# A pair of squares added on GpSimd ahead of the sums that TensorE makes for an RMS norm

## The chip, the core and the metric

The kernel runs on one core of a Trainium2 chip. The metric is the device time of one execution in microseconds. The core has five engines with instruction queues of their own, which meet only at semaphores: TensorE (PE in the profile; PEld is its weight load), VectorE (DVE), ScalarE (ACT), GpSimd (POOL) and SyncE (SP), which issues most of the DMAs.

## What is computed

Two small models in a row, for one sequence of 256 tokens of width 1024: two hybrid layers (latent attention, a gated delta rule and block attention side by side), a last norm, and then four layers, each with a feed-forward part, a mixer (HGRN2, mLSTM, sliding-window attention, HGRN2), a second feed-forward part and a gated projection. Ahead of each of these parts stands an RMS norm. What the change touches is the mean of squares in it:

```python
def rmsnorm_2(x, gain):
    xf = x.astype(jnp.float32)
    y = xf * lax.rsqrt(jnp.mean(xf * xf, axis=-1, keepdims=True) + EPS)
    return (y * gain.astype(jnp.float32)).astype(x.dtype)

def swiglu(x, w_gu, w_down):
    g, u = jnp.split(x @ w_gu, 2, axis=-1)
    return (jax.nn.silu(g) * u) @ w_down
```

Everything is in float32.

## The kernel before

The activations lie transposed: `x` is 128 partitions (of the width) by 8 tiles by 256 tokens. All products with weights are made in three matmuls of 128x128 by 256, from a high and a low part of either operand (`with_hi`, `with_lo`, L137 to L146). The weights come in 781 chunks of 512 KB through a ring; ACT makes the high part of a chunk (`hi`, L92), DVE the low part (`lo`, L100), five chunks ahead of TensorE.

A norm isn't waited for. TensorE multiplies the unscaled `x` times gain, and the root of the mean square scales the product afterwards. On the way from the residual `x` to that root (class `Norm` and the four functions behind it):

- ACT squares the tiles of `x` into `xn` (`square`, L219), right behind the high part of each tile (`split_hi`, L206).
- DVE adds the squares of tiles 0 to 5 down to one tile in three steps (`fold_six`, L246, L250, L253).
- TensorE sums over the partitions: `sum_squares` (L370) takes each 128x128 half of a tile of squares as weights, with a column of ones as the moving operand. It sums three tiles: 0, 6 and 7. A matmul of plain float32 stands in the trace as two records, so three tiles of two halves are 12 records.
- ACT takes the mean (`root_in`, L383), GpSimd the power -0.5 (`spread_root`, L397), TensorE spreads it over the partitions (`rstd_rows`, L410), and DVE copies it (`take_rstd`, L418). Then DVE scales the first product (L555), ACT makes the SiLU (L527), DVE the product (L559), ACT its high part (L531), DVE its low part (L564), for which the first down-projection `down` waits (L452).

Norms with the sum of three tiles follow a `finish` of `OutProjection` (six: one per hybrid layer and one per mixer) and a `ple` with a next layer (three). The one behind the second hybrid layer also serves the last norm of the first model: class `Inner` squares `x` a second time, folds it and sums another three tiles (L323). The other norms square in two big pieces and sum one tile; they aren't touched.

The order on each engine is the order in which the functions write their blocks. On GpSimd that is, behind a mixer's out-projection: `split_p` (L618, a cast, and L620, a subtraction, both 128x512, for the gated projection far behind), and then the power of `spread_root`. `split_p` is written after the out-projection, but waits only for things that are long done there.

## Time and profile before

| | us |
|---|---|
| median of 3 runs | 2420.28 |
| lowest, highest | 2419.44, 2424.91 |
| profiled execution, its own time | 2427.05 |
| span of the profiled execution | 2425.2 |

The engines' busy times are TensorE 2410.8 us, DVE 1725.1, ACT 1317.8 and GpSimd 91.4. In the rows, a number such as L370 is the line of the kernel; times count from the start of the span. The granted clock of TensorE is at its full level in all 40 slices of the span. TensorE's matmuls overlap: a record of a matmul of 256 columns is 0.28 us long, while the next starts 0.11 us after it, so distances between starts count there, not lengths.

### The profile page before, as it was taken

Reading aid. Unit: us, or ns where it says so; the run is one execution under the profiler, and the core shown is the slowest. Engines: PE = TensorE matmul, PEld = TensorE weight load, DVE = VectorE, ACT = ScalarE, POOL = GpSimd, SP = SyncE. Lnnn points to the kernel's source line nnn. Section 1 sums busy time; section 2 is a strip of 40 time slices with the busy share of each in tenths; the row PEclk is TensorE's granted clock in tenths of the full one; section 3 lists DMA queues with packets and bytes.
Section 4 is the critical chain, followed back from the end, with each engine's and each line's share of the span. In section 5 each row is a group of like instructions: output and inputs, shape, how many; then the busy total and the mean of one; then the engine's idle time right before and its main releaser. Section 6 shows DMA issues by size and latency. Waiting matters only on the chain.

```text
span 2425.2 us, 51808 instructions
## 1 busy us (share of the span) xinstructions
PE 2410.8 (99%) x20462; PEld 2381.4 (98%) x20462; DVE 1725.1 (71%) x2422; ACT 1317.8 (54%) x2019; POOL 91.4 (4%) x91
## 2 busy tenths in 40 slices
PE   9999999999999999999999999999999999999999
PEld 9999999999999999999999999998999999999999
DVE  8878867568776677667766676687667766877666
ACT  5756755446564465445544554466445544765444
POOL 1000000001200000000000000000000000220000
PEclk9999999999999999999999999999999999999999
DMA  7315326555456556655465566543655655535563
GB/s 267 114 62 174 122 67 221 183 185 170 131 174 194 190 180 201 195 185 182 136 203 188 170 210 196 191 140 124 203 194 178 197 197 191 166 123 190 191 194 127
DMA packets 115378, 418.86 MB, mean 173 GB/s; under 512 B 12832, under 2 KB 14112, under 8 KB 114976
## 3 DMA queue, kind: packets, MB, share of 16 engines
q1 hardware_dynamic: 114096, 412.40, 52.2%
q8 instruction: 109, 1.79, 0.3%
q0 software_dynamic: 560, 2.10, 0.3%
q10 hardware_dynamic: 576, 2.27, 0.2%
q14 instruction: 37, 0.30, 0.0%
HBM read 414.62 MB, written 2.10 MB: 172 GB/s over the span
## 4 chain that ended last, share of the span: by engine, by line
PE 94%; DVE 3%; ACT 1%; DMA 0%; issue 0%; ACTq 0%; SPq 0%; DVEq 0%
PE ps_gu L140 18%; PE ps_gu L146 17%; PE ps_gu L141 17%; PE ps_acc L140 9%; PE ps_acc L146 8%; PE ps_acc L141 8%; PE ps_acc L2709 1%; PE ps_acc L2270 1%; PE ps_misc L140 1%; DVE w_lo L100 1%; PE ps_gu L2306 1%; PE ps_misc L141 1%; PE ps_misc L146 1%; PE ps_sum L140 1%; PE ps_sum L146 1%; PE ps_sum L141 1%
## 5 line engine op out<-in xcount | busy, mean ns | idle before, releaser
L100 DVE TENSOR_TENSOR w_lo<-w_raw,w_hi 128x1024 fp32r<-128x1024 f32 x781 | 953.2, 1228 | 382.6 <-ACT w_hi L92 377.8
L140 PE MATMUL ps_gu<-xn_hi,w_hi 128*128 128x256 f32 x3832 | 1057.9, 280 | 2.2 <-DVE x_res L1342 0.8
L141 PE MATMUL ps_gu<-xn_hi,w_lo 128*128 128x256 f32 x3832 | 1047.0, 277 | 0.0
L92 ACT ACTIVATE w_hi<-w_raw 128x1024 fp32r<-128x1024 f32 x781 | 819.7, 1056 | 362.7 <-PE ps_gu L146 269.1
L146 PE MATMUL ps_gu<-xn_lo,w_hi 128*128 128x256 f32 x3832 | 1010.7, 277 | 0.0
L140 PEld LDWEIGHTS ps_gu<-xn_hi,w_hi 128*128 128x128 f32 x3832 | 719.9, 188 | 5.8 <-issue 2.5
L141 PEld LDWEIGHTS ps_gu<-xn_hi,w_lo 128*128 128x128 f32 x3832 | 720.2, 188 | 0.3
L146 PEld LDWEIGHTS ps_gu<-xn_lo,w_hi 128*128 128x128 f32 x3832 | 697.3, 188 | 0.0
L140 PE MATMUL ps_acc<-h_hi,w_hi 128*128 128x256 f32 x1496 | 415.1, 278 | 0.0
L146 PE MATMUL ps_acc<-h_lo,w_hi 128*128 128x256 f32 x1496 | 413.6, 276 | 0.0
L141 PE MATMUL ps_acc<-h_hi,w_lo 128*128 128x256 f32 x1496 | 413.5, 276 | 0.0
L527 ACT ACTIVATE silu<-ps_gu 128x256 f32<-128x256 f32 x176 | 67.7, 384 | 425.8 <-DVE ps_gu L555 425.8
L140 PEld LDWEIGHTS ps_acc<-h_hi,w_hi 128*128 128x128 f32 x1496 | 280.7, 188 | 0.3
L146 PEld LDWEIGHTS ps_acc<-h_lo,w_hi 128*128 128x128 f32 x1496 | 280.8, 188 | 0.0
L141 PEld LDWEIGHTS ps_acc<-h_hi,w_lo 128*128 128x128 f32 x1496 | 280.8, 188 | 0.0
L555 DVE TENSOR_TENSOR ps_gu<-ps_gu,rstd 128x512 f32<-128x512 f32 x176 | 123.0, 699 | 62.0 <-PE ps_gu L146 61.7
L559 DVE TENSOR_TENSOR h<-silu,ps_gu 128x256 f32<-128x256 f32 x176 | 74.1, 421 | 90.0 <-ACT silu L527 90.0
L140 PE MATMUL ps_acc<-xn_hi,w_hi 128*128 128x256 f32 x336 | 95.1, 287 | 0.5 <-DVE xn L3422 0.5
L141 PE MATMUL ps_acc<-xn_hi,w_lo 128*128 128x256 f32 x336 | 92.1, 278 | 0.0
L397 POOL TENSOR_TENSOR rstd_columns<-mean_square_columns,powers 128x2 f32<-128x2 f32 x17 | 18.9, 1112 | 1891.6 <-ACT mean_square_columns L383 1891.6
L146 PE MATMUL ps_acc<-xn_lo,w_hi 128*128 128x256 f32 x336 | 87.0, 278 | 0.0
L564 DVE TENSOR_TENSOR h_lo<-h,h_hi 128x256 fp32r<-128x256 f32 x176 | 74.0, 420 | 7.7 <-ACT h_hi L531 7.7
(462 smaller groups left out, 2637.6 us busy)
## 6 DMA issues: line engine op xcount, KB each, us to landing
w_raw<-in_w_dram SPq DMA_DIRECT2D x781, 512.0 KB, 4.1
const<-in_const_dram SPq DMA_DIRECT2D x1, 1216.0 KB, 8.6
distance_rows<-arena POOLq DMA_DIRECT2D x1, 1024.0 KB, 6.5
p_all<-distance_rows POOLq DMA_DIRECT2D x2, 512.0 KB, 5.3
p_all<-in_p_dram ACTq DMA_DIRECT2D x1, 1024.0 KB, 6.4
out_dram<-x_res SPq DMA_DIRECT2D x8, 128.0 KB, 1.9
x_res<-in_x_dram ACTq DMA_DIRECT2D x1, 512.0 KB, 6.7
x_res<-in_x_dram SPq DMA_DIRECT2D x1, 512.0 KB, 6.1
```

Source lines behind the costliest of these rows:

```text
L92: act.activation(self.w_hi[:, s, :], self.w_raw[:, r, :], ACT.Copy).then_inc(self.w_hi_ready.sem, 1)
L100: dve.tensor_tensor(self.w_lo[:, s, :], self.w_raw[:, c % NR, :], self.w_hi[:, s, :], ALU.subtract)\
L140: pe.matmul(out, self.w_hi[:, s, j0:j0 + width], rhs_hi, start=start, stop=False, skip_group_check=True)
L141: pe.matmul(out, self.w_lo[:, s, j0:j0 + width], rhs_hi, start=False, stop=False, skip_group_check=True)
L146: return pe.matmul(out, self.w_hi[:, s, j0:j0 + width], rhs_lo, start=False, stop=last, skip_group_check=True)
L527: act.activation(k.s[:, t % 2, :], k.ps_gu[t % 2][:, 0:S], ACT.Silu).then_inc(silu.sem, 1)
L555: dve.tensor_tensor(gu, gu, k.rstd[:, :].unsqueeze(1).to_broadcast([P, 2, S]), ALU.mult).then_inc(sc.sem, 1)
L559: dve.tensor_tensor(k.h[:, t % 2, :], k.s[:, t % 2, :], k.ps_gu[t % 2][:, S:2 * S], ALU.mult)\
L564: dve.tensor_tensor(k.h_lo[:, t % 2, :], k.h[:, t % 2, :], k.h_hi[:, t % 2, :], ALU.subtract)\
L2270: mm = pe.matmul(at_bank(acc01, n), four(Lm[lv % 2])[:, n, :], four(T)[:, n, :], start=(n % 4 == 0), stop=True, skip_group_check=True)
L2306: mm = pe.matmul(gub(n), four(U)[:, n, :], four(Y)[:, n, :], start=(n % 4 == 0), stop=True, skip_group_check=True)
L2709: mm = pe.matmul(ps[:, h * P:(h + 1) * P], lhs(h), rhs(h), start=(h == 0), stop=True, skip_group_check=True)
```

## The change

The diff below is shortened. The squares of tiles 6 and 7 are added on GpSimd into tile 6 (`fold_pair`), as soon as the last square is made, and `sum_squares` sums tiles 0 and 6. It waits for that addition (`pair_folded`) in place of the squares. `Inner` gets the same. The new blocks are written behind the out-projection or the gated projection, and so ahead of `split_p`.

```diff
-        self.tiles = (0,) if squares < KD else (0, 6, 7)
+        self.tiles = (0,) if squares < KD else (0, 6)
...
+    def fold_pair(self):
+        k, xn = self.k, self.k.xn
+        @k.block.gpsimd
+        def _(pool):
+            pool.wait_ge(*k("square_made").at(self.squares))
+            pool.tensor_tensor(xn[:, 6, :], xn[:, 6, :], xn[:, 7, :], ALU.add).then_inc(*k("pair_folded").up())
+
     def made(self):
-        self.k.take(self.b, self.h0, self.l0, 1)
-        self.k.summed = self.tiles, self.k("square_made").at(self.squares)
+        k = self.k
+        k.take(self.b, self.h0, self.l0, 1)
+        if len(self.tiles) == 1:
+            k.summed = self.tiles, k("square_made").at(self.squares)
+        else:
+            self.fold_pair()
+            k.summed = self.tiles, k("pair_folded").made()
...
+    def fold_pair(self):
+        k, squares = self.k, self.squares
+        @k.block.gpsimd
+        def _(pool):
+            pool.wait_ge(*k("inner_square_made").at(KD))
+            pool.tensor_tensor(squares[:, 6, :], squares[:, 6, :], squares[:, 7, :], ALU.add)\
+                .then_inc(*k("inner_pair_folded").up())
     def sum(self, pe):
...
-        pe.wait_ge(*k("inner_square_made").at(KD))
-        for m in (0, 6, 7):
+        pe.wait_ge(*k("inner_pair_folded").at(1))
+        for m in (0, 6):
...
         nxt.made()
+        if inner:
+            inner.fold_pair()
```

TensorE, at the sum behind a gated projection (`ps_gu0` and `ps_gu1` are the banks of the first two feed-forward tiles), before:

```order
L146 MATMUL ps_gu0<-xn_lo1,w_hi 128x256 [waits xn_lo_ready]
L146 MATMUL ps_gu0<-xn_lo1,w_hi 128x256
L370 MATMUL ps_sum<-ones,xn 128x1 [waits square_made,squares_folded,misc_free]
L370 MATMUL ps_sum<-ones,xn 128x1 x5
L140 MATMUL ps_gu1<-xn_hi1,w_hi 128x256 [waits w_lo_ready,ple_gate_ready]
```

and after the change:

```order
L146 MATMUL ps_gu0<-xn_lo1,w_hi 128x256 [waits xn_lo_ready]
L146 MATMUL ps_gu0<-xn_lo1,w_hi 128x256
L394 MATMUL ps_sum<-ones,xn 128x1 [waits pair_folded,squares_folded,misc_free]
L394 MATMUL ps_sum<-ones,xn 128x1 x3
L140 MATMUL ps_gu1<-xn_hi1,w_hi 128x256 [waits w_lo_ready,ple_gate_ready]
```

Two of six matmuls (four of twelve records) are gone, and the wait is for the addition in place of the squares.

GpSimd, behind the second mixer (mLSTM), before; `rstd_columns` is the power of `spread_root`, once for the norm ahead of the mixer and then for the one behind it:

```order
L397 TENSOR_TENSOR rstd_columns<-mean_square_columns,powers 128x2 [waits mean_sq_col]
L613 UNCONDITIONAL_BRANCH
L618 CAST h_hi<-p_all 128x512 [waits chunk_done,p_loaded]
L620 TENSOR_TENSOR h_lo<-p_all,h_hi 128x512 [waits p_hi_ready]
L391 UNCONDITIONAL_BRANCH
```

and after the change:

```order
L421 TENSOR_TENSOR rstd_columns<-mean_square_columns,powers 128x2 [waits mean_sq_col]
L242 UNCONDITIONAL_BRANCH
L245 TENSOR_TENSOR xn<-xn 128x256 [waits square_made]
L637 UNCONDITIONAL_BRANCH
L642 CAST h_hi<-p_all 128x512 [waits chunk_done,p_loaded]
L644 TENSOR_TENSOR h_lo<-p_all,h_hi 128x512 [waits p_hi_ready]
L415 UNCONDITIONAL_BRANCH
```

The addition stands ahead of the cast and the subtraction of `split_p`, with a wait for the last square. These two follow it from now on, at all four mixers.

## Rows read from the trace of the kernel before

**Rows 1.** The page: busy times, and the chain that ended last by engine

```profile
PE 2410.8 (99%) x20462; PEld 2381.4 (98%) x20462; DVE 1725.1 (71%) x2422; ACT 1317.8 (54%) x2019; POOL 91.4 (4%) x91
PE 94%; DVE 3%; ACT 1%; DMA 0%; issue 0%; ACTq 0%; SPq 0%; DVEq 0%
```

**Rows 2.** Waits of TensorE, first of twelve: us in total, times, longest

```profile
PE ps_sum L140 <- ACT xn_hi L1235: 2.1, 2, 1.0
```

**Rows 3.** Instructions of L370: ns min/median/max, first and last start, form

```profile
L370 PE MATMUL ps_sum<-ones,xn x144: 164/250/250, 17.8 to 2402.0; 128*128 128x1 f32 x144
```

**Rows 4.** Timeline of TensorE, inner sum: start us, us, line, operation, out<-in, count

```profile
376.24 1.48 PE L323 MATMUL ps_sum<-ones,arena 128*128 128x1 f32 x12
377.58 0.36 PE L140 MATMUL ps_gu<-xn_hi,w_hi 128*128 128x256 f32 x1
```

**Rows 5.** Groups by form, POOL and DVE: busy us, mean ns, idle before

```profile
L2256 POOL TENSOR_TENSOR arena<-arena,const 128x1024 f32<-128x1024 f32 x4 | 9.5, 2372 | 177.5 <-PE ps_acc L2270 177.5
L100 DVE TENSOR_TENSOR w_lo<-w_raw,w_hi 128x1024 fp32r<-128x1024 f32 x781 | 953.2, 1228 | 382.6 <-ACT w_hi L92 377.8
```

**Rows 6.** Timelines of POOL and DVE, at the first and second split_p

```profile
642.45 0.61 POOL L618 CAST h_hi<-p_all 128x512 fp32r<-128x512 f32 x1
643.14 1.69 POOL L620 TENSOR_TENSOR h_lo<-p_all,h_hi 128x512 fp32r<-128x512 f32 x1
643.00 0.68 DVE L2692 TENSOR_TENSOR arena<-arena 128x512 f32<-128x512 f32 x1
643.59 2.32 DVE L100 TENSOR_TENSOR w_lo<-w_raw,w_hi 128x1024 fp32r<-128x1024 f32 x1
1101.85 1.30 POOL L620 TENSOR_TENSOR h_lo<-p_all,h_hi 128x512 fp32r<-128x512 f32 x1
```

**Rows 7.** Timelines behind the first gated projection: ACT, DVE, PE, PEld

```profile
912.32 0.40 ACT L219 ACTIVATE xn<-x_res 128x256 f32<-128x256 f32 x1
913.90 0.43 DVE L253 TENSOR_TENSOR xn<-xn 128x256 f32<-128x256 f32 x1
914.25 4.62 DVE L100 TENSOR_TENSOR w_lo<-w_raw,w_hi 128x1024 fp32r<-128x1024 f32 x4
918.88 0.42 DVE L418 COPY rstd<-ps_sum 128x256 f32<-128x256 f32 x1
921.39 0.42 DVE L564 TENSOR_TENSOR h_lo<-h,h_hi 128x256 fp32r<-128x256 f32 x1 [0.48 <-ACT h_hi L531]
915.35 1.39 PE L370 MATMUL ps_sum<-ones,xn 128*128 128x1 f32 x12
922.33 0.19 PEld L140 LDWEIGHTS ps_acc<-h_hi,w_hi 128*128 128x128 f32 x1
```

**Rows 8.** Timelines behind the first mixer's out-projection: ACT, DVE, PEld

```profile
701.35 0.40 ACT L219 ACTIVATE xn<-x_res 128x256 f32<-128x256 f32 x1
701.22 1.22 DVE L100 TENSOR_TENSOR w_lo<-w_raw,w_hi 128x1024 fp32r<-128x1024 f32 x1
702.35 0.69 DVE L250 TENSOR_TENSOR xn<-xn 128x512 f32<-128x512 f32 x1
702.96 0.48 DVE L211 SCALAR_TENSOR_TENSOR xn_lo<-x_res,vec,xn_hi 128x256 fp32r<-128x256 f32 x1
703.35 0.42 DVE L253 TENSOR_TENSOR xn<-xn 128x256 f32<-128x256 f32 x1
705.66 1.42 PEld L370 LDWEIGHTS ps_sum<-ones,xn 128*128 128x128 f32 x12
707.20 0.26 ACT L383 ACTIVATE mean_square_columns<-ps_sum,eps 128x2 f32<-128x2 f32 x1 [2.25 <-PE ps_sum L370]
708.45 1.23 DVE L100 TENSOR_TENSOR w_lo<-w_raw,w_hi 128x1024 fp32r<-128x1024 f32 x1 [2.41 <-ACT w_hi L92]
```

**Rows 9.** Timeline of DVE behind the two hybrid layers' sums

```profile
201.73 0.42 DVE L418 COPY rstd<-ps_sum 128x256 f32<-128x256 f32 x1 [5.26 <-PE ps_sum L410]
379.06 1.23 DVE L100 TENSOR_TENSOR w_lo<-w_raw,w_hi 128x1024 fp32r<-128x1024 f32 x1 [2.95 <-ACT w_hi L92]
```

## What the change should do to the time

> **What bounds the kernel now.** I read the page first: TensorE is busy for 2410.8 of 2425.2 us and holds 94% of the chain that ended last, while GpSimd works for 91.4 us [rows 1]. Then TensorE's own waits: twelve rows, the longest in total 2.1 us, about 10 us in all [rows 2]. So time that goes out of TensorE's queue is time of the kernel, unless TensorE then comes too early to something that another engine makes. That is read at each place of the change from timelines: when the last square ends, what DVE does until the root is there, and when the first down-projection wants its operand.
>
> **What is removed.** L370 has 144 records in 18 norms [rows 3]. Nine of these norms sum three tiles, 12 records each, and nine sum one, 4 records each: 108 and 36, which is 144. The inner norm has another 12 [rows 4]. The change takes 4 records out of each of ten sums, 40 in all. A record costs what it holds the next one back: 12 of them run from 376.24 to the 377.58 of the next L140, 1.34 us or 0.112 each [rows 4]. Four are 0.45 us, and 40 are **4.47 us**, if nothing gives any of it back. This is the bound above of the saving.
>
> **What is added.** Ten additions of 128x256 on GpSimd. No such row is in the trace. The nearest are the same operation with 1024 columns, 2.37 us [rows 5], and L620 with 512, 1.30 us where DVE leaves it alone [rows 6]. A straight line through the two gives 0.23 us and 1.07 per 512 columns, so 0.77 us for 256. GpSimd has nothing else to do there, and the sum comes 2.6 to 4 us behind the last square: 912.72 to 915.35 behind a gated projection [rows 7], 701.75 to 705.66 behind a mixer [rows 8]. By itself the addition is hidden everywhere.
>
> It isn't by itself, since DVE is at work in that stretch, and the two get in each other's way. Rows 6 show it. L620 of GpSimd wants to start at 643.14, when DVE's L2692 runs (until 643.68). It takes 1.69 us in place of 1.30, so it waits for L2692. DVE's next instruction, an L100 that begins at 643.59, takes 2.32 us in place of 1.228 [rows 5]: it is held for 1.09 us. All three read two operands from SBUF. So GpSimd gets its turn when DVE's running instruction ends, even with another of DVE's right behind, and holds that next one for its record less 0.21 us (1.30 - 1.09). For the new addition that is 0.77 - 0.21 = 0.56 us, about half of 1.09. For the cast (0.61 us) I estimate 0.40. A hold can't be below zero; its bound above is the whole record.
>
> **The three sums behind gated projections.** The last square ends at 912.72. DVE is busy without a gap from there to the copy of the root at 918.88 (the fold, then four L100 from 914.25 to 918.87), and from there the chain of the first feed-forward tile runs to the h_lo of L564, which ends at 921.81 [rows 7]. TensorE loads the first weights of that down-projection at 922.33. The slack is 0.52 us. Now TensorE comes 0.45 us earlier, at 921.88, and DVE 0.47 to 0.56 us later (the copy waited some hundredths for TensorE before), so h_lo is ready at 922.28 to 922.37. TensorE waits until then and starts where it started before. **0 us** each (between -0.1 and +0.02 with this hold), out of 0.45. What hid the addition was slack that the saving itself uses up. The fold ends at 914.33, and 914.9 is still ahead of the sum.
>
> **The four sums behind mixers.** Here DVE idles for 2.41 us ahead of the L100 at 708.45, because that waits for an ACT instruction which stands behind L383, and L383 waits for the sum [rows 8]. So the chain to the root starts from the sum and moves with it, and the down-projection sees no new slack or want. What can be late is the sum itself. The addition brings `split_p` behind it: three instructions on GpSimd in a row. They start at 701.8 and take turns with DVE. The addition gets in behind the L100 that ends at 702.44 and holds L250 by 0.56. The cast gets in behind L250 and holds L211 by 0.40. L620 gets in behind L211 and holds L253 by 1.09. L253, the last step of the fold, ended at 703.77 and now ends at 703.77 + 2.05 = 705.82. The sum loads its first weights at 705.66. It waits 0.16 us, so that 0.29 of 0.45 are left: **1.2 us** for four. DVE's two L100 behind the fold then end at about 708.2, just where the next one may start (708.45 less 0.29), so nothing more is lost. If one of the three falls into a gap of DVE, the loss is 0; hence 0 to 0.16.
>
> **The two sums of the hybrid layers.** DVE idles 5.26 us ahead of the root's copy in the first, and 2.95 us ahead of the next L100 in the second [rows 9]; both wait for things behind the sum. Nothing of `split_p` follows. The inner norm has two additions, 1.1 us of DVE, inside these 2.95. The saving stays: 0.45 for one sum and 0.89 for two. The fill of the arena with zeros (L1697, L1698) moves behind the first addition; it reads nothing, and is wanted only behind the root.
>
> **The sum**: 0.45 + 0.89 + 4 x 0.29 + 3 x 0 = 2.5 us. The profiled execution would have a span of 2422.7 in place of 2425.2, and an own time of 2424.5 in place of 2427.05. That execution lies 6.8 us above the median of the runs, 2420.28; I carry the difference over to the median: **2417.7 us**.
>
> **The rivals.**
>
> *All of it stays* (GpSimd's turns fall into DVE's gaps, or the copy at 918.88 has more room than it seems): 4.47 us, 2415.8. For it: DVE's instructions have gaps of some hundredths where a step of the fold waits for the last one. Against it: the row with 2.32 us. 20%.
>
> *The hold is dearer than the row.* If DVE is held for the whole GpSimd instruction, it is 0.77, 0.61 and 1.30 us. Behind gated projections the down-projection then starts 0.2 us later than before, 3 x -0.2. Behind mixers the fold ends at 703.77 + 2.68 = 706.45, 0.79 behind 705.66, so each loses 0.34. With 1.34 from the hybrid layers the sum is -0.7 us: 2421.0. Against it: 1.09 is less than 1.30 in the rows. 13%. The Trainium skill has this rule (SBUF — State Buffer, "Who interferes with whom"): a DVE instruction with two SBUF inputs and a GpSimd instruction that reads SBUF exclude each other, and the one that comes second is blocked until the other is through. By that page the change would gain nothing. The trace agrees with the exclusion, and its 1.09 us beside 1.30 says that the block is shorter than the instruction.
>
> *The saving comes back at every feed-forward part*, as a wait ahead of the first down-projection, and only the first sum, which no feed-forward part follows, keeps it: 0.45 us, 2419.8. Against it: the 2.41 us of idle DVE that end with the sum. 6%.
>
> *GpSimd finds no turn* (slower). If DVE keeps its operand path as long as it has the next instruction in its queue, the addition runs only when DVE's row of instructions ends. Behind a gated projection that is 918.87, and the sum is made at 919.4 in place of 915.24: 4.2 us, three times. Behind a mixer two L100 end at about 706.2, and the sum starts 1.1 us late, four times; the inner norm loses about 2. Together 12.6 + 4.4 + 2 - 4.5 = 14.5 us: 2434.8. It decides from where an addition waits for its turn for over 1.86 us behind a gated projection (2.63 us of room less its own 0.77). Against it: GpSimd did get in ahead of the L100 at 643.59. 5%.
>
> **How the numbers follow.** Forecast 56%, the rivals 20, 13, 6 and 5. A measurement of this kernel can tell about 0.2% from no change, 4.8 us, so faster begins at 2415.4. Faster: two in five of the first rival, whose 4.47 us lie just inside, and a little of the forecast by scatter, 12%. Slower: the last rival and a bit of the second, 6%. Within: 82%. The three runs before lie 5.5 us apart, so scatter counts beside the cases. The range takes in the first rival (2415.8) and the second (2421.0), 2415.0 to 2421.2, and leaves out the last and some scatter.
>
> **What would show it.** In the trace of the changed kernel: 8 records per touched sum, 16 for the two of the inner norm; the new addition at 0.77 us, or more where it waits; one DVE instruction behind it longer by 0.56; behind gated projections an h_lo that ends about 0.5 us later against the sum's start than before, and a short wait of TensorE ahead of `ps_acc`; behind mixers cast and subtraction ahead of the sum, L253 stretched by a microsecond, and the sum's first load waiting for it by 0.1 to 0.2 us; behind hybrid layers no wait. The prediction is wrong if DVE isn't stretched at all, if the additions end behind the sum's place, or if TensorE's rows outside these places change.

## The result and the profile after

The changed kernel takes **2448.95 us** (median of 15 runs, 2424.97 to 2458.14); the kernel before took 2424.16 us beside it (15 runs, 2416.88 to 2435.05). The ratio is 1.0087, with a 95% interval of 1.007 to 1.0104: slower by nearly 1%. The prediction, 2417.7 us (2415.0 to 2421.2), is wrong in sign, and the time lies far outside the range. The profiled execution took 2451.54 us with a span of 2449.7 us; it answers to the 2427.05 and 2425.2 of before.

The page of the changed kernel: busy times, the chain by engine, and TensorE's three groups of gate and up matmuls (the columns are those of [rows 1] and [rows 5]).

```profile
PE 2434.8 (99%) x20422; PEld 2403.9 (98%) x20422; DVE 1732.9 (71%) x2422; ACT 1318.3 (54%) x2019; POOL 105.8 (4%) x101
PE 92%; DVE 4%; ACT 2%; DMA 1%; issue 1%; POOL 0%; ACTq 0%; SPq 0%; DVEq 0%
L140 PE MATMUL ps_gu<-xn_hi,w_hi 128*128 128x256 f32 x3832 | 1065.3, 282 | 2.3 <-DVE x_res L1366 0.8
L141 PE MATMUL ps_gu<-xn_hi,w_lo 128*128 128x256 f32 x3832 | 1049.7, 278 | 0.0
L146 PE MATMUL ps_gu<-xn_lo,w_hi 128*128 128x256 f32 x3832 | 1013.8, 278 | 0.0
```

TensorE has the 40 records less that the change takes out (20462 in [rows 1]), and yet it is busy for 24.0 us more. No group of the page stands out: the three groups of 3832 have the same counts as before and means of 278 to 282 ns, and the idle column is as good as empty. The waits of TensorE hardly differ either. These are the first row, which is that of [rows 2], and the two rows that are new (us in total, times, longest):

```profile
PE ps_sum L140 <- ACT xn_hi L1259: 2.1, 2, 1.0
...
PE ps_sum L434 <- POOL rstd_columns L421: 0.6, 2, 0.3
...
PE ps_acc L140 <- DVE h_lo L588: 0.2, 1, 0.2
```

So 0.8 us of new waits stand beside 24.5 us of longer span. Where the time is can be seen if one counts TensorE's instructions in stretches of equal length, each in the middle of one of the eight feed-forward parts. The columns: the stretch, its us, then for PE, PEld, DVE, ACT and POOL the busy us with the number of instructions, then the granted clock, the DMA share and GB/s. First the kernel before (parts 1 to 4):

```profile
410.00:550.00 140.00, 140.00 (x1180) 140.00 (x1179) 84.11 (x100) 62.37 (x84) 0.00 (x0) 1.00 0.56 185
720.00:860.00 140.00, 140.00 (x1238) 140.00 (x1237) 88.57 (x105) 63.99 (x85) 0.00 (x0) 1.00 0.62 198
940.00:1080.00 140.00, 140.00 (x1238) 140.00 (x1237) 87.94 (x104) 65.35 (x88) 0.00 (x0) 1.00 0.62 195
1230.00:1370.00 140.00, 140.00 (x1238) 140.00 (x1237) 88.02 (x104) 64.43 (x87) 0.00 (x0) 1.00 0.61 193
```

and the changed kernel (all eight parts in their order):

```profile
400.00:540.00 140.00, 140.00 (x1237) 140.00 (x1237) 88.73 (x105) 65.59 (x88) 0.00 (x0) 1.00 0.61 199
720.00:860.00 140.00, 140.00 (x1179) 140.00 (x1179) 83.65 (x100) 61.69 (x83) 0.00 (x0) 1.00 0.56 185
940.00:1080.00 140.00, 140.00 (x1238) 140.00 (x1237) 88.18 (x104) 65.22 (x87) 0.00 (x0) 1.00 0.60 196
1230.00:1370.00 140.00, 140.00 (x1180) 140.00 (x1179) 83.66 (x100) 61.80 (x83) 0.00 (x0) 1.00 0.57 185
1440.00:1580.00 140.00, 140.00 (x1238) 140.00 (x1237) 89.26 (x105) 64.81 (x87) 0.00 (x0) 1.00 0.62 200
1720.00:1860.00 140.00, 140.00 (x1180) 140.00 (x1179) 84.73 (x99) 61.72 (x83) 0.00 (x0) 1.00 0.56 182
1930.00:2070.00 140.00, 140.00 (x1180) 140.00 (x1179) 84.82 (x99) 61.75 (x83) 0.00 (x0) 1.00 0.58 189
2260.00:2400.00 140.00, 140.00 (x1238) 140.00 (x1237) 88.36 (x105) 64.55 (x86) 0.00 (x0) 1.00 0.61 193
```

A part has one of two rates, and nothing between them: 1238 matmuls in 140 us, which is one in 113 ns, or 1180, one in 119. The granted clock is 1.00 in all of them, TensorE never idles, GpSimd does nothing there, and DVE, ACT and the DMA have slightly less to do in the slower ones, because TensorE asks for less. Before, one part of eight had the wide spacing (the first); after, four have it (parts 2, 4, 6 and 7). From the first SiLU of a part to its last, the 21 steps take 166.1 to 166.8 us at the narrow spacing and 174.0 to 174.7 at the wide one. Three more wide parts at 8.2 us are 24.6 us, and the span grew by 24.5. **The loss lies in the spacing of whole parts, not at the ten sums.** That the two numbers agree to a tenth is in part chance. Counted from the start of one norm's sum to the start of the next, a wide part is 8 to 9 us longer than a narrow one in the same place, and part 3 of the changed kernel, wide only at its beginning, is 0.9 us longer; against that stand some 1.6 us that the change does save, as the runs at the end show. The single times of the changed kernel show the groups too: they cluster at 2425, 2432, 2441, 2450 and 2458 us, in steps of about eight.

### The profile page after: what moved, and what is told of

Read it like the earlier page. It is cut to its first block, busy times and chain, and to the rows that moved or that the text cites. A ratio compares the mean times of both kernels' runs of the same rounds, so it can differ in the third digit from the quotient of the medians.

```text
span 2449.7 us, 51738 instructions
## 1 busy us (share of the span) xinstructions
PE 2434.8 (99%) x20422; PEld 2403.9 (98%) x20422; DVE 1732.9 (71%) x2422; ACT 1318.3 (54%) x2019; POOL 105.8 (4%) x101
## 4 chain that ended last, share of the span: by engine, by line
PE 92%; DVE 4%; ACT 2%; DMA 1%; issue 1%; POOL 0%; ACTq 0%; SPq 0%; DVEq 0%
PE ps_gu L140 17%; PE ps_gu L146 17%; PE ps_gu L141 17%; PE ps_acc L140 8%; PE ps_acc L146 8%; PE ps_acc L141 8%; PE ps_acc L2735 1%; DVE w_lo L100 1%; PE ps_acc L2296 1%; DMA w_raw<-in_w_dram 1%; PE ps_misc L140 1%; PE ps_gu L2332 1%; PE ps_misc L141 1%; PE ps_misc L146 1%; PE ps_sum L140 1%
## 5 line engine op out<-in xcount | busy, mean ns | idle before, releaser
L100 DVE TENSOR_TENSOR w_lo<-w_raw,w_hi 128x1024 fp32r<-128x1024 f32 x781 | 952.3, 1226 | 387.8 <-ACT w_hi L92 382.5
L140 PE MATMUL ps_gu<-xn_hi,w_hi 128*128 128x256 f32 x3832 | 1065.3, 282 | 2.3 <-DVE x_res L1366 0.8
L141 PE MATMUL ps_gu<-xn_hi,w_lo 128*128 128x256 f32 x3832 | 1049.7, 278 | 0.0
L140 PEld LDWEIGHTS ps_gu<-xn_hi,w_hi 128*128 128x128 f32 x3832 | 719.1, 188 | 6.1 <-issue 2.7
L141 PEld LDWEIGHTS ps_gu<-xn_hi,w_lo 128*128 128x128 f32 x3832 | 720.0, 188 | 0.3
L140 PE MATMUL ps_acc<-h_hi,w_hi 128*128 128x256 f32 x1496 | 419.3, 280 | 0.2 <-DVE h_lo L588 0.2
L141 PE MATMUL ps_acc<-h_hi,w_lo 128*128 128x256 f32 x1496 | 414.9, 277 | 0.0
L140 PEld LDWEIGHTS ps_acc<-h_hi,w_hi 128*128 128x128 f32 x1496 | 280.3, 187 | 1.2 <-DVE h_lo L588 1.0
L141 PEld LDWEIGHTS ps_acc<-h_hi,w_lo 128*128 128x128 f32 x1496 | 280.7, 188 | 0.0
L140 PE MATMUL ps_acc<-xn_hi,w_hi 128*128 128x256 f32 x336 | 94.8, 286 | 0.5 <-DVE xn L3448 0.5
L141 PE MATMUL ps_acc<-xn_hi,w_lo 128*128 128x256 f32 x336 | 92.0, 278 | 0.0
L588 DVE TENSOR_TENSOR h_lo<-h,h_hi 128x256 fp32r<-128x256 f32 x176 | 74.0, 420 | 7.7 <-ACT h_hi L555 7.7
```

The source lines that it names most:

```text
L100: dve.tensor_tensor(self.w_lo[:, s, :], self.w_raw[:, c % NR, :], self.w_hi[:, s, :], ALU.subtract)\
L140: pe.matmul(out, self.w_hi[:, s, j0:j0 + width], rhs_hi, start=start, stop=False, skip_group_check=True)
L141: pe.matmul(out, self.w_lo[:, s, j0:j0 + width], rhs_hi, start=False, stop=False, skip_group_check=True)
L588: dve.tensor_tensor(k.h_lo[:, t % 2, :], k.h[:, t % 2, :], k.h_hi[:, t % 2, :], ALU.subtract)\
```

## What the two spacings are

These are records of TensorE as read from the trace: start, line, distance to the record before it in ns, and by how much its weight load leads it. They follow the spreading of the root over the partitions (L410 before, L434 after), which comes some 3 us behind the sum: two matmuls of 128 columns that need the power of GpSimd. Behind the first mixer, before:

```
708.774 L146 d119 lead 116
708.889 L410 d115 lead  99    spreading, not waited for
708.997 L410 d108 lead 107
709.024 L140 d27  lead  25
709.227 L141 d203 lead 120
709.345 L146 d118 lead 115
709.462 L140 d117 lead 115
709.578 L141 d116 lead 113
709.692 L146 d114 lead 110
709.805 L140 d113 lead 110    from here 113, 114, 113 for 169 us
```

and after:

```
699.080 L146 d119 lead 116
699.234 L434 d154 lead   3    spreading, waited for
699.393 L434 d159 lead 107
699.421 L140 d28  lead  26
699.625 L141 d204 lead 120
699.751 L146 d126 lead 123
699.866 L140 d115 lead 112
699.984 L141 d118 lead 114
700.104 L146 d120 lead 118
700.222 L140 d118 lead 116    from here 117 to 120, now and then 124, for 187 us
```

In both kernels TensorE comes out of the sum at the wide spacing (the 119 in the first lines). The spreading ends that in the kernel before. Where TensorE has to wait for the spreading's operand, the wide spacing often stays, and then it stays to the end of the part. The wait itself is some hundredths of a microsecond here: the load starts 3 ns ahead of its matmul in place of 99, and the matmul comes 154 ns behind the record before it in place of 115. At parts 4, 6 and 8 this distance is 613, 505 and 176 ns. So parts 2, 4 and 6, which are wide, were waited for, and so was part 8, which is narrow. Part 7 is wide without a wait at its spreading (117 ns, load 98 ns ahead), and part 3 begins wide in the same way.

What made it wait is in the timelines of GpSimd and DVE behind the first mixer, after. Their counterparts before are [rows 8], and for the power the row that stands last here (from the kernel before):

```profile
692.40 1.20 POOL L245 TENSOR_TENSOR xn<-xn 128x256 f32<-128x256 f32 x1 [59.33 <-ACT xn L219]
693.56 1.07 POOL L642 CAST h_hi<-p_all 128x512 fp32r<-128x512 f32 x1
694.71 1.36 POOL L644 TENSOR_TENSOR h_lo<-p_all,h_hi 128x512 fp32r<-128x512 f32 x1
697.85 1.33 POOL L421 TENSOR_TENSOR rstd_columns<-mean_square_columns,powers 128x2 f32<-128x2 f32 x1 [1.78 <-ACT mean_square_columns L407]
...
691.79 1.22 DVE L100 TENSOR_TENSOR w_lo<-w_raw,w_hi 128x1024 fp32r<-128x1024 f32 x1
692.93 1.23 DVE L265 TENSOR_TENSOR xn<-xn 128x512 f32<-128x512 f32 x1
694.08 0.83 DVE L211 SCALAR_TENSOR_TENSOR xn_lo<-x_res,vec,xn_hi 128x256 fp32r<-128x256 f32 x1
694.83 1.52 DVE L268 TENSOR_TENSOR xn<-xn 128x256 f32<-128x256 f32 x1
696.27 3.71 DVE L100 TENSOR_TENSOR w_lo<-w_raw,w_hi 128x1024 fp32r<-128x1024 f32 x3
```

```profile
707.54 0.69 POOL L397 TENSOR_TENSOR rstd_columns<-mean_square_columns,powers 128x2 f32<-128x2 f32 x1 [62.71 <-ACT mean_square_columns L383]
```

The two engines take turns just as the prediction has it. The addition waits for the L100 that ends at 693.01. The fold's first step (L265, L250 before) takes 1.23 us in place of 0.69, so it is held for 0.54 (forecast 0.56); L211 0.83 in place of 0.48, 0.35 (0.40); the last step L268 1.52 in place of 0.42, 1.10 (1.09). The fold ends at 696.35 and the sum starts at 696.45, 212 ns behind the record before it where it was 116: a wait of 0.10 us (forecast 0.16). Then comes what the prediction left out: three L100 run without a gap from 696.27, and the **power** on GpSimd, two columns of numbers, is itself a reader of SBUF. It is free to go at 697.85, when the second L100 runs, and ends at 699.18, 1.33 us later in place of 0.69. At the second and third mixer it takes 1.79 and 1.68 us: it comes within 0.1 us of the start of an L100 and waits for all of it. TensorE, which comes 0.45 us sooner for its shorter sum, wants it at about 699.1.

## The experiments

Three theories. **W**: a wait of TensorE within a feed-forward part's first microseconds, however short, can leave it at the wide spacing for the whole part. **F**: the shorter sum does it, by its number of small matmuls. **G**: GpSimd's additions do it, by their use of SBUF. The first four kernels take the change apart and make W's wait with nothing of the change in it.

**Two tiles summed and no addition** (kernel before; the squares of tile 7 are left out of the mean):

```diff
-        self.tiles = (0,) if squares < KD else (0, 6, 7)
+        self.tiles = (0,) if squares < KD else (0, 6)
...
-        for m in (0, 6, 7):
+        for m in (0, 6):
```

> The kernel before, with the squares of tile 7 left out of the sums that take three tiles (the mean of squares is that of seven tiles): 8 records of small matmuls in place of 12 at ten places, no addition on GpSimd. In the trace of the changed kernel four of eight feed-forward parts run at 118.9 ns per matmul in place of 113.3 and are 8.2 us longer each; in that of before it is one. Theory W (a short wait of TensorE ahead of or behind the spreading of the root throws the part into the slow spacing): no wait arises here, so at most one or two parts are slow and the time is 3 to 5 us below before, ratio 0.998 to 0.9985. Rival F (it is the smaller number of small matmuls that leaves TensorE in the slow spacing): four parts slow, ratio about 1.01. Rival G (GpSimd's additions disturb): as W here.

Measured: 2425.5 us (12 runs, 2415.9 to 2441.99) beside 2419.8; ratio 1.0036 (1.001 to 1.0063). So all three theories missed: W and G forecast less time than before, and F four wide parts. The profiled execution (2424.9 us, span 2422.8) has one wide part, the third. A wait that I had not expected, and that the kernel before doesn't have, stands among TensorE's:

```profile
PE ps_sum L410 <- POOL rstd_columns L397: 0.5, 3, 0.2
```

It comes at the three sums behind gated projections. There the power is held by an L100 before as well. The power behind the first gated projection, before and with two tiles summed:

```profile
917.12 1.17 POOL L397 TENSOR_TENSOR rstd_columns<-mean_square_columns,powers 128x2 f32<-128x2 f32 x1 [24.31 <-ACT mean_square_columns L383]
```

```profile
906.49 1.62 POOL L397 TENSOR_TENSOR rstd_columns<-mean_square_columns,powers 128x2 f32<-128x2 f32 x1 [24.28 <-ACT mean_square_columns L383]
904.07 4.62 DVE L100 TENSOR_TENSOR w_lo<-w_raw,w_hi 128x1024 fp32r<-128x1024 f32 x4
```

It starts 0.45 us sooner against the four L100 and takes 0.45 us longer: the power ends when that L100 lets it, and TensorE, which arrives 0.45 us sooner than before, waits for it: its record comes 444 ns behind the last one. Three waits (parts 3, 5 and 7), one wide part: less than W in its strict form wants. But no part without a wait is wide, and five of the 12 runs lie at 2440.7 to 2442.0 us, some 26 above the 2415.43 that this kernel takes below with every profiled part narrow: by their time, all three parts were wide there. A shorter sum alone makes the kernel no faster, though it loses 40 records.

**Additions only**, three tiles still summed (changed kernel otherwise; the additions write a spare tile, and the sums wait for them as in the changed kernel):

```diff
-        self.tiles = (0,) if squares < KD else (0, 6)
+        self.tiles = (0,) if squares < KD else (0, 6, 7)
...
-            pool.tensor_tensor(xn[:, 6, :], xn[:, 6, :], xn[:, 7, :], ALU.add)
+            pool.tensor_tensor(k.spare[:, :], xn[:, 6, :], xn[:, 7, :], ALU.add)
```

> The kernel before with the ten additions on GpSimd, written into a spare tile, and TensorE waiting for them; the sums still take three tiles, 12 records. GpSimd's order is that of the changed kernel, cast and subtraction included. Theory W: the root behind the mixers is late by as much as in the changed kernel, less the 0.45 us by which TensorE comes later; the power there ends at 2.7 us behind the start of the sum, and TensorE wants it at 3.1, so it just isn't waited for, and the sums of the gated projections have their slack back: one to three slow parts, ratio 1.000 to 1.005. Rival G (the additions themselves slow the part): four slow parts, 1.01 to 1.015. Rival F: no more than before, 1.000.

Measured: 2450.66 us (6 runs, 2445.55 to 2464.36), ratio 1.0138 (1.0115 to 1.0161). Its page lists `PE ps_sum L439 <- POOL rstd_columns L426: 0.8, 3, 0.3` among TensorE's waits, again behind the gated projections, and the parts behind those three (3, 5, 7) are wide, all others narrow. The three waits are W's, but the time is what G had forecast (1.01 to 1.015) and W had not (up to 1.005): I had expected the gated projections' slack to cover the addition. F falls here: the number of small matmuls is that of before. G is left beside W, since the additions are in both.

**`split_p` written ahead of the mixer**, so that its cast and subtraction no longer stand behind the addition (changed kernel otherwise):

```diff
+            split_p(k, layer)
...
-            split_p(k, layer)
```

> The changed kernel, with split_p written ahead of the mixer in place of behind it, so that GpSimd has its cast and subtraction behind it when the addition comes. Theory W: behind the four mixers DVE is held by 0.56 us only, the power isn't late, TensorE doesn't wait at the spreading, and those four parts are fast; the three behind gated projections stay as in the changed kernel (one or two slow). Time 15 to 20 us below the changed kernel, ratio to before 1.000 to 1.004. Rivals F and G: as the changed kernel, 1.0087.

Measured: 2425.5 us (12 runs, 2416.66 to 2433.86), ratio 1.0025 (1.001 to 1.004), 23 us less than the changed kernel for the place of two instructions on GpSimd. All four parts behind mixers are narrow. In the profiled execution (span 2429.8) parts 1 and 5 are wide. TensorE waits for `h_lo` behind gated projections instead, `PE ps_acc L140 <- DVE h_lo L588: 1.6, 3, 0.6`. The two instructions haven't gone away: ahead of the mixer they stand right behind the power of the norm behind a gated projection, and there they hold DVE (these are the rows of part 3; in the changed kernel the four L100 take 4.62 us):

```profile
914.94 1.08 POOL L642 CAST h_hi<-p_all 128x512 fp32r<-128x512 f32 x1
916.10 2.16 POOL L644 TENSOR_TENSOR h_lo<-p_all,h_hi 128x512 fp32r<-128x512 f32 x1
912.06 5.04 DVE L100 TENSOR_TENSOR w_lo<-w_raw,w_hi 128x1024 fp32r<-128x1024 f32 x4
```

The wait for `h_lo` is about the same at the three places (the matmul behind it comes 858, 855 and 754 ns behind the last), and what it does is not: part 3 is narrow ahead of it and behind it, part 5 is narrow ahead and wide behind, part 7 wide ahead and narrow behind. The additions are all still there, so G can't be the whole of it.

**A late root and nothing else** (kernel before, with two fills of a spare tile on GpSimd between the mean and the power, at the eight feed-forward parts):

```diff
 def spread_root(k, n=None, late=False):
...
+        if late:
+            for _ in range(2):
...
+                pool.memset(k.spare[:, :], 0.0).then_inc(*k("spare_written").up())
...
-    spread_root(k)
+    spread_root(k, late=True)
```

> The kernel before, untouched but for two fills of a spare 128x256 tile on GpSimd between the wait for the mean and the power, at the eight feed-forward parts. Fills read nothing, so DVE isn't held; the root comes 0.6 to 0.8 us later. TensorE had 0.55 us of room behind mixers and some tenths behind gated projections, so it waits 0.1 to 0.8 us per part, 3 us in all. Theory W: four or more of eight parts fall into the slow spacing: 2450 us, ratio 1.008 to 1.02. Rivals F and G: only the waits themselves, ratio 1.001 to 1.002.

Measured: 2457.26 us (4 runs, 2456.38 to 2459.52), ratio 1.0151 (1.0134 to 1.0168). TensorE's wait and the stretches inside parts 3, 4 and 5:

```profile
PE ps_sum L415 <- POOL rstd_columns L402: 3.2, 4, 0.9
```

```profile
940.00:1080.00 140.00, 140.00 (x1180) 140.00 (x1180) 83.50 (x98) 61.20 (x81) 0.00 (x0) 1.00 0.57 185
1230.00:1370.00 140.00, 140.00 (x1238) 140.00 (x1237) 88.37 (x104) 64.30 (x86) 0.00 (x0) 1.00 0.59 193
1440.00:1580.00 140.00, 140.00 (x1180) 140.00 (x1179) 84.71 (x100) 62.22 (x83) 0.00 (x0) 1.00 0.58 187
```

Parts 3, 5, 7 and 8 are wide. No sum is shortened and nothing is added to anything, yet with 3.2 us of waits the kernel takes 37 us more. (A little of the profiled execution is another matter: from 370 to 390 us the granted clock is 0.80 and 0.86, with records 213 ns apart, the 1.2 GHz level, after 10 us in which TensorE was busy for 8.70. It costs about 3 us in part 1.) **That is W**: a late root is enough, without the shorter sum and without the additions. The kernel has two fills on GpSimd besides, ahead of every part. They aren't what decides: parts 2, 4 and 6 have them and are narrow, and the two tiles above have no fill and a wide part behind a wait. And a short wait alone isn't a sentence: at parts 2, 4 and 6 the matmul comes 143 or 144 ns behind the last in place of 115, and they stay narrow; part 8 (167 ns) and parts 3, 5 and 7 (1133 ns) turn wide.

**How often.** From the traces of seven kernels (before, after, the four above and the one with additions at mixers only, below), I took parts 2 to 8 and sorted them by whether the load of the spreading came 2 or 3 ns ahead of its matmul (it waited) or 60 to 99 ns (it didn't), and by the spacing of the records right behind:

```
                       narrow   wide
not waited for            29      3
waited for                 6     11
```

So a wait isn't a verdict but a draw, and it went the wrong way in about two of three, against one in eleven without it. The later wait for `h_lo` is a draw too, as the three parts with `split_p` first show. In the changed kernel it leaves part 5 narrow and part 7 wide. Part 3 comes out of the sum wide, stays so over a first wait for `h_lo`, and turns narrow within eight records behind a second one of 0.2 us at 930.2: a wait can also free it. The first part has two spreadings, its own and the inner norm's; among the seven kernels it ends wide in three (before, `split_p` first, additions at mixers only), with no wait at all. In these three the stream was narrow (113 ns) ahead of the first spreading and wide behind it, and one of the 3 in the table above, part 7 with `split_p` first, is the same case: the spreading that mostly ends a wide stretch begins one there.

**A way out of it.** This is an order of matmuls in which the wide spacing might not last. In tiles 1 and 2 of each part (the second and third), for the up-projection, the eight pairs with `xn_hi` are issued first and then the eight with `xn_lo` (the same matmuls in another order):

```diff
+                pairs = t in (1, 2) and n == 1
+                if pairs:
+                    for j in range(KD):
+                        k.with_hi(...)
                 for j in range(KD):
...
+                    if pairs:
+                        mm = k.with_lo(...)
+                        continue
```

I applied it to the kernel before, and to the kernel with the late root:

> The kernel before, with the matmuls of the up-projection in the second and third feed-forward tile in another order: first all sixteen with the high part of x, then the eight with its low part, as the first tile has them. The same matmuls, none more or less. In the traces so far the first tile nearly always runs at 113.3 ns, also where 118.9 came in. If this order is what brings the fast spacing back, no feed-forward part is slow (also the first, which is slow in the profile of before): 2415 to 2418 us, less scatter, ratio 0.997 to 0.999. If it doesn't matter: ratio 0.999 to 1.001 and the scatter of before.

> The same order of matmuls in the kernel with the late root (two fills ahead of the power), which ran at 2457 us. If the 37 us there are the slow spacing of whole feed-forward parts, this one falls to before plus the waits themselves: 2418 to 2425 us. If they come from the wait or from GpSimd in another way, it stays at 2450 or more. If the order of the matmuls doesn't bring the fast spacing back, it also stays.

Measured: before with this order, 2418.64 us (12 runs, 2416.43 to 2420.22) beside 2420.45, ratio 0.9987 (0.9976 to 0.9997), and its runs lie within 3.8 us where those of the kernel before beside it (33 runs) lie within 11.8. The median is 0.6 us over the range that I had given, the ratio is in it. The late root goes from 2457.26 to 2424.16 us (2421.32 to 2425.25), ratio 1.0004 (0.9992 to 1.0015). The same stretches of the late root with this order:

```profile
940.00:1080.00 140.00, 140.00 (x1237) 140.00 (x1237) 87.99 (x103) 64.27 (x86) 0.00 (x0) 1.00 0.59 193
1230.00:1370.00 140.00, 140.00 (x1237) 140.00 (x1237) 88.17 (x104) 63.98 (x85) 0.00 (x0) 1.00 0.59 193
1440.00:1580.00 140.00, 140.00 (x1238) 140.00 (x1237) 88.37 (x103) 63.98 (x85) 0.00 (x0) 1.00 0.60 194
```

TensorE still waits for the root there (2.6 us in three waits and 1.2 us in one). Beside the kernel before in the same order that is 5.5 us by the medians and 3.5 by the profiled spans (2419.2 and 2415.7). The 33 us between the two kernels with the late root are the spacing's: the fills and the waits are in both. How it turns is to be seen in the records of the changed kernel with this order, at the first part (start, line, distance, lead):

```
386.825 L141 d114 lead 112
386.944 L140 d119 lead 116
387.062 L141 d118 lead 115
387.180 L140 d118 lead 116
387.297 L141 d117 lead 114
387.417 L140 d120 lead 116
387.536 L141 d119 lead 115
387.649 L140 d113 lead 110    from here on 113, 113, 114
```

Six pairs of L140 and L141 pass at the wide spacing, then it falls to 113 inside the row of pairs.

**The change and its halves, with the draw taken out.** The same order on the changed kernel, on the sum without additions, on the additions without the sum, and on the changed kernel with `split_p` first:

> The changed kernel itself, with the order of matmuls that keeps every feed-forward part in the fast spacing; to be held against the kernel before with that order (2418.6 us). What is left is the change without its lottery: this is where the prediction's own sum, 2.5 us saved, can be read: 2416.1. If the waits of TensorE at the root's spreading and at the first down-projection cost more than the prediction took, it is 2417 to 2419; above 2420 something else is in it.

> Two tiles in place of three with nothing added (tile 7 is left out of the mean of squares), in that order: the price of 40 small records. By 0.112 us each 4.5 us are saved, less some 0.25 us at each of three gated projections, where GpSimd's power waits for the same DVE instruction as before and TensorE now waits for it: 3.7 us under 2418.6, so 2414.9. If the first of these waits isn't there, 2414.1; if the small records cost less than their spacing, 2416 or more.

> The ten additions with three tiles summed, in that order. With every part fast, the additions cost what TensorE waits for: 0.3 us at the four mixers' roots and up to 0.5 at three gated projections, 1 to 2.5 us above 2418.6: 2419.6 to 2421.1, where the same kernel without the order ran at 2450.66. If additions slow TensorE in another way than through the slow spacing, it stays above 2440.

> The changed kernel with split_p ahead of the mixer, in that order. Against the changed kernel in that order it has only the addition on GpSimd behind a mixer, so the waits at four mixers' sums and roots go, 0.2 to 0.4 us each: 0.8 to 1.6 us less than the first run of this call, and above the kernel with additions at out-projections only (2414.86) by 0 to 0.6 us.

Measured, 12 runs each, all parts narrow in each profiled execution, the kernel before at 2418.73 beside them; the first line repeats the kernel before with this order from above, for comparison (it was measured beside 2420.45):

```
                               median   lowest   profiled span   ratio (95%)
before, this order             2418.64  2416.43  2415.7          0.9987 (0.9976 to 0.9997)
changed kernel, this order     2416.89  2415.33  2414.1          0.9981 (0.9966 to 0.9995)
two tiles, no addition         2415.43  2413.34  2413.5          0.9976 (0.9960 to 0.9992)
additions, three tiles         2420.16  2417.19  2421.7          0.9993 (0.9977 to 1.0009)
changed kernel, split_p first  2416.28  2414.40  2414.3          0.9988 (0.9971 to 1.0005)
```

The changed kernel goes from 2448.95 to 2416.89 us, 32 us for an order of matmuls. Against the kernel before in the same order the change is worth 1.75 us by the medians, 1.6 by the spans and 1.1 by the lowest runs; the two weren't measured side by side, and the intervals of the ratios overlap, so this is a size and not a proof. The forecast was 2416.1, from 2.5 us saved. The shorter sum alone saves 3.2 us by the medians and 2.2 by the spans, and the additions alone cost 1.5 by the medians. (The span of the additions alone is no measure: from 370 to 390 us the granted clock is 0.90 and 0.93 there, with records 213 ns apart.) With the additions at 2420.16 us in this order and at 2450.66 without it, G falls as a cost of its own. `split_p` first gives another 0.6 by the medians and nothing by the spans (2414.3 beside 2414.1), within what can't be told; the 0.8 to 1.6 that I had forecast leave out that TensorE now waits 1.7 us for `h_lo` behind the gated projections, where its cast and subtraction stand. One run of it stands apart at 2431.76, as one of the two tiles does at 2421.69. The first is 15.5 us over its median, as much as two wide parts would add. Neither was profiled, so whether the order of pairs always brings the narrow spacing back is open. What is left of the waits in the changed kernel with this order is small:

```profile
PE ps_acc L140 <- DVE h_lo L596: 0.3, 2, 0.2
...
PE ps_sum L434 <- POOL rstd_columns L421: 0.3, 1, 0.3
```

**The version that is best.** This is the changed kernel with the additions only where they save something, at the six sums behind out-projections (seven additions with the inner norm's); the gated projections keep three tiles and no addition, and `split_p` goes first. Once without and once with the order of pairs:

```diff
-    nxt = None if next_gain is None else Norm(k, next_gain)
+    nxt = None if next_gain is None else Norm(k, next_gain, pair=False)
...
-        self.tiles = (0,) if squares < KD else (0, 6)
+        self.tiles = (0,) if squares < KD else (0, 6) if pair else (0, 6, 7)
```

> The same without the new order of matmuls. Theory W: a saving of 3.1 us at each number of slow parts, and about as many slow parts as in before: ratio 0.998 to 1.001. If additions as such throw parts into the slow spacing: ratio 1.003 or more.

> The additions at the six sums behind out-projections only, the three sums behind gated projections with three tiles as before, split_p ahead of the mixer, and the order of matmuls of the two runs above. By theory W there is nothing left that TensorE waits for: 7 of 10 savings of 0.45 us, 3.1 us below the other order on the kernel before: 2412 to 2416 us, ratio 0.996 to 0.998. Rival: something else in the additions costs time; then it is above 2418.

Measured: without the order 2415.64 us (12 runs, 2412.52 to 2424.5), ratio 0.9977 (0.9964 to 0.9991); with it 2414.86 us (10 runs, 2413.74 to 2415.75), ratio **0.997 (0.9957 to 0.9983)**. Neither has a wait for the root or for `h_lo` in its rows. The eight faster of the 12 runs without the order lie at 2412.5 to 2416.4, the other four at 2422.4 to 2424.5; the profiled one is among these, and its first part is wide (174.5 us). With the order the ten runs lie within 2.0 us. It beats both kernels: 5.6 us less than the kernel before beside it and some 34 less than the changed one. Of the 5.6 the order of pairs gives 1.8, and the change at these six places 3.8 by the medians and 1.8 by the spans (2415.7 and 2413.9; forecast 3.1).

## Why the prediction was wrong

**What bounds the kernel** was right (TensorE's queue), but not read to its end. "Time that goes out of TensorE's queue is time of the kernel" takes for granted that each record has a fixed price. In the feed-forward parts, some 1,470 records each from the first SiLU to the last, the record turned out to have two.

**What is removed** was sized rightly, 0.112 us a record: with the order of pairs, the two tiles without additions save 3.2 us by the medians (2.2 by the spans), inside the 4.47 given as the bound above, and what is missing is lost where TensorE waits for the power behind gated projections. The two sums behind the second hybrid layer show the full size: from there to the next norm's sum it is 183.65 us in place of 184.55, 0.90 less (forecast 0.89).

**What is added** was right in its mechanism and its sizes: 0.54, 0.35 and 1.10 us of hold against 0.56, 0.40 and 1.09. The Trainium skill's rule that a DVE instruction with two SBUF inputs and a GpSimd instruction that reads SBUF exclude each other (SBUF — State Buffer, "Who interferes with whom") agrees with this trace; the block is again shorter than the blocking instruction (1.10 beside 1.36 us).

**Behind gated projections** the forecast was 0 us, because `h_lo` is later by about what the sum saves. It is: in the changed kernel h_lo ends at 921.28 and the down-projection's load starts at 921.34 (921.81 and 922.33 in the kernel before, [rows 7]); the new wait is 0.2 us. As a sum this was right: in the order of pairs, where the spacing is out of it, the stretch from the first such sum to the next norm's is 182.69 us in the kernel before and 182.71 in the changed one. But I priced this wait at nothing on the ground that it only fills up time that was saved.

**Behind mixers** stands the first step that failed: "so nothing more is lost". The prediction has DVE's two L100 behind the fold end at about 708.2 and looks only at who comes next on DVE. It doesn't ask what GpSimd wants in that stretch. The power (L397) would have been due at 707.54 less 0.29, inside the second L100 by the prediction's own times, and the exclusion that it had just worked out for the additions applies to it. The row for it was in the trace: the power takes 0.69 us behind mixers and 1.17 behind gated projections, where L100 run. Taken at its length this is little: in the changed kernel TensorE's wait for the power is 0.04, 0.50, 0.39 and 0.06 us at the four mixers. In the order of pairs it is 0.04 at three of them and 0.42 at the fourth, and where it is 0.04, the stretch from the sum to the next norm's is 184.66 us in place of 184.96 or 185.38 in the kernel before with the same order: at least 0.30 saved, where the prediction had 0.29. At the fourth it is 185.07, and nothing is saved.

**The price of a wait** is the second failure, and the one that makes the prediction wrong in sign. "TensorE waits until then and starts where it started before" (0 us each, behind gated projections) and "It waits 0.16 us" (1.2 us saved in all, behind mixers) take a wait of TensorE at its length, and so the sum of 2.5 us saved has no term for what the stream does behind a wait. Behind the spreading of the root, waits of 0.03 to 0.9 us decided over 8.2 us each, and the changed kernel has four wide parts in place of one: a span 24.5 us longer in place of 2.5 shorter. The kernel before showed that there are two spacings: its first part took 174.5 us for the steps that the other seven did in 166.2 to 166.5, with the same instructions. And the three runs that "lie 5.5 us apart" were entered in the prediction as scatter. The 15 runs of the comparison, which it didn't have, show seven at 2416.9 to 2420.3 and then none until 2424.2. A question as to what those 5.5 us are would have led there.

**The rivals.** None of them describes what came. The one on the slower side was a long wait of the additions for their turn (2434.8 us); no addition waited so. The 6% for slower was too little: every rival was a sum of local waits, and none asked what would happen if the cost weren't local. That the order of pairs brings the time to 2416.89 us, inside the stated range, doesn't make the prediction right; it shows that its local sum was sound and that the step from there to the kernel's time was not.

**What stays open.** Why TensorE has two spacings for the same stream, and what decides the draw. That a wait can bring on the wide spacing is shown; how three of 32 parts came wide without one, part 7 of the changed kernel among them, is not. Where the spreading wasn't waited for in parts 2 to 8, its first record came 115 ns behind the one before it in all 29 cases that turned narrow; of the three that turned wide two had 116 and 117 ns, and the third 115 out of a narrow stream. That points to the phase in which the small matmuls meet the stream, and is no more than an observation. Nor did a run try fewer than two tiles of pairs, or pairs behind the sum itself.

## What to carry to other kernels

When an engine that bounds a kernel runs a long stream without a gap, count its instructions per 100 us in each stage before anything else, for several executions: two rates in like stages mean that there is a state, and that the cost of a small wait isn't its length. Runs that group in equal steps are a sign of it, not noise. And when two engines exclude each other on SBUF, list all instructions of both in the stretch, the tiny ones too: the one that decided here has two columns.

## What the runs showed of the hardware

- The same stream of 128x128 by 128x256 matmuls in three passes runs at 113.3 or at 118.9 ns per record, at a granted clock of 1.00, with weight loads that lead by 110 ns or by 115 to 122. Either holds for about 170 us and more, 1,500 records, and the next break of the stream ends it.
- Ahead of the spreading, behind the sum's one-column matmuls, the stream was wide in 48 of the 49 parts (2 to 8 of seven kernels). The two matmuls of 128 columns led back in 29 of 32 without a wait and in 6 of 17 with one.
- With rows of eight pairs that share a moving operand (`xn_hi`), in two tiles of each part, none of the 56 parts of seven profiled executions was wide; two runs that weren't profiled lie 6.3 and 15.5 us over the medians of their kernels.
- A 128x2 power on GpSimd takes 0.69 us beside an idle DVE and 0.77 to 1.79 us beside L100 of DVE, by how much of the L100 is left when it comes; it ends some 0.55 us behind the end of the L100 that held it.
